# Plain writes in the two turns of the substituted blocks, strided reads in what uses them

## The reference

```
def step(s, inp):                       # one token, one head
    r_t, w_t, k_t, v_t, kk_t, a_t = inp
    sa = einsum('bhvk,bhk->bhv', s, -kk_t)
    s = s * w_t + sa * (kk_t * a_t) + v_t * k_t
    return s, einsum('bhvk,bhk->bhv', s, r_t)
```

## Time and profile before

| | |
|---|---|
| median of three runs | 4666.56 us (4660.83 to 4667.1) |
| profiled execution, its own time | 4672.97 us |
| its span | 4671.2 us |
| mean granted clock of TensorE | 0.863 of full speed |
| PE busy, matmuls | 3689.4 us, 79% |
| DVE busy | 1769.3 us, 38% |
| ACT busy | 776.1 us, 17% |

### The profile page before, as it was taken

How to read it: one execution, slowest core, us unless ns; L and a number is a source line. 1 busy time by engine, 2 the same in 40 slices (tenths; PEclk the granted TensorE clock), 3 DMA queues, 4 the chain that set the end, 5 groups by cost and what they waited for, 6 DMA issues and landing times. The chain is left out here.

```text
span 4671.2 us, 51101 instructions
## 1 busy us (share of the span) xinstructions
PE 3689.4 (79%) x21012; PEld 2181.8 (47%) x21012; DVE 1769.3 (38%) x3454; ACT 776.1 (17%) x1454; POOL 60.1 (1%) x77
## 2 busy tenths in 40 slices
PE   5788778877877888886997577785978879758995
PEld 2355445544655545544443432233444444437884
DVE  2466655665563646644001300002142321332112
ACT  1223222322230211111000100001121121200011
POOL 0000000000000000000000000000000000000000
PEclk7888788888867998988998599996989999867997
DMA  3110110011101010003102599972010000026884
GB/s 130 74 51 15 64 64 35 30 64 51 45 20 51 27 48 34 27 28 153 54 36 81 197 428 428 428 316 103 39 75 36 38 36 39 36 78 259 334 330 166
DMA packets 73151, 530.80 MB, mean 114 GB/s; under 512 B 23248, under 2 KB 24656, under 8 KB 46096
## 3 DMA queue, kind: packets, MB, share of 16 engines
q1 hardware_dynamic: 66064, 503.01, 27.1%
q0 software_dynamic: 4608, 16.78, 1.0%
q10 hardware_dynamic: 2304, 8.39, 0.4%
HBM read 500.81 MB, written 27.34 MB: 113 GB/s over the span
## 5 line engine op out<-in xcount | busy, mean ns | idle before, releaser
L1740 PE MATMUL ex_ps<-ex_ring,ex_xs 128*64 128x512 f32 x1024 | 241.1, 626 | 66.7 <-DMA ex_ring<-expert_slabs_in 63.7
L2477 PEld LDWEIGHTS ge_ps<-ge_xeT,ge_ring 128*128 128x128 f32 x2048 | 233.7, 194 | 10.5 <-issue 10.5
L2477 PE MATMUL ge_ps<-ge_xeT,ge_ring 128*128 128x128 f32 x2048 | 234.0, 277 | 2.9 <-DVE ge_xeT L2535 2.9
L1974 PE MATMUL mh_ps<-mh_w,xmT 128*128 128x512 f32 x512 | 223.1, 596 | 8.6 <-ACT mh_sg L1997 8.6
L692 PE MATMUL rw_ps<-hT,rw_w 128*128 128x512 f32 (+1 forms) x560 | 218.0, 535 | 0.0
L1125 PE MATMUL sg_ps<-hTp,sg_w 128*128 128x512 f32 x384 | 180.7, 626 | 27.9 <-PEq L61 27.9
L1740 PEld LDWEIGHTS ex_ps<-ex_ring,ex_xs 128*64 128x64 f32 x1024 | 87.3, 144 | 220.0 <-issue 218.1
L1974 PEld LDWEIGHTS mh_ps<-mh_w,xmT 128*128 128x128 f32 x512 | 97.6, 191 | 133.5 <-issue 121.5
L528 PE MATMUL rw_ps<-rw_tk,cs 128*2 128x512 f32 (+2 forms) x384 | 152.6, 560 | 0.0
L692 PEld LDWEIGHTS rw_ps<-hT,rw_w 128*128 128x128 f32 x560 | 104.8, 196 | 77.0 <-issue 68.4
L1965 PE MATMUL mh_ps<-xmT,mh_w_ahead 128*128 128x512 f32 x256 | 120.7, 636 | 22.5 <-PEq L61 22.5
(11 more groups left out here) (584 smaller groups left out, 5902.4 us busy)
## 6 DMA issues: line engine op xcount, KB each, us to landing
ex_ring<-expert_slabs_in SPq DMA_DIRECT2D x96, 2048.0 KB, 17.3
ge_ring<-expert_slabs_in SPq DMA_DIRECT2D x48, 2048.0 KB, 13.1
rw_tk<-mod_w_in SPq DMA_DIRECT2D x8, 3072.0 KB, 15.4
rw_tk<-ada_in SPq DMA_DIRECT2D x8, 2048.0 KB, 9.3
mh_w_ahead<-head_slabs_in SPq DMA_DIRECT2D x8, 2048.0 KB, 10.8
mh_w<-head_slabs_in SPq DMA_DIRECT2D x8, 2048.0 KB, 10.3
rw_w<-rw_slabs_in SPq DMA_DIRECT2D x8, 1536.0 KB, 6.5
sg_w<-xbc_slabs_in SPq DMA_DIRECT2D x4, 3072.0 KB, 10.4
```

Source lines behind the costliest of these rows:

```text
L1740: mm = pe.matmul(ps[halves[j], bank, :], src[:, k, halves[j]], ring[:, (n + j) % RING, k, :], start=k == 0, stop=k == KC - 1)
L1974: mm = pe.matmul(ps[:, 4 + t, :], xmT[:, k, P * t:P * t + P], w[1 + n // 4][:, k, :], start=k == 0, stop=k == KC - 1)
L2477: mm = pe.matmul(ps[:, 2 + 2 * (j % 2) + n, P * f:P * f + P], w[:, k, P * f:P * f + P], xeT[:, j, k, :], start=k == 0, stop=k == KC - 1)
```

## The change

Both turns write in plain order: `by_row` is now indexed `[c, u]` and `by_col` `[i, u]`, and everything that reads one unit of them reads with a stride of 32 numbers. The number of instructions, their order, their waits and their results are the same.

```
-  mm = pe.matmul(ps[hi, bank, ...], near[lo, u, 32:64], by_row[lo, u, :], start=True, stop=True)
+  mm = pe.matmul(ps[hi, bank, ...], near[lo, u, 32:64], by_row[lo, :, u], start=True, stop=True)
...
-  mm = pe.matmul(ps[lo, 5, at], mid[hi, u, :], by_col[hi, u, :], start=True, stop=True)
+  mm = pe.matmul(ps[lo, 5, at], mid[hi, u, :], by_col[hi, :, u], start=True, stop=True)
...
-  mm = pe.matmul(ps[hi, 5, at], by_col[hi, u, :], mid[hi, u, :], start=True, stop=True)
+  mm = pe.matmul(ps[hi, 5, at], by_col[hi, :, u], mid[hi, u, :], start=True, stop=True)
...
-  act.copy(xt[quarter(x), of_dir(d), quarter(x % 2)], src[quarter(x), of_dir(d), :]).then_inc(s.xt_ready, 1)
+  act.copy(xt[quarter(x), of_dir(d), quarter(x % 2)], src[quarter(x), :, of_dir(d)].rearrange("p i u -> p u i")).then_inc(s.xt_ready, 1)
...
-  dve.transpose(by_row[:, :, :].rearrange("p u c -> p c u"), xb[:, :, :].rearrange("p i c -> p c i")).then_inc(s.turned, 1)
-  dve.transpose(by_col[:, :, :].rearrange("p u i -> p i u"), xb[:, :, :]).then_inc(s.turned, 1)
+  dve.transpose(by_row[:, :, :], xb[:, :, :].rearrange("p i c -> p c i")).then_inc(s.turned, 1)
+  dve.transpose(by_col[:, :, :], xb[:, :, :]).then_inc(s.turned, 1)
```

More of the change, by code:

```diff
@@ L743, in _ @@
                         bank = 7 if u < 16 else 4
-                        mm = pe.matmul(ps[hi, bank, 32 * (u % 16):32 * (u % 16) + 32], near[lo, u, 32:64], by_row[lo, u, :], start=True, stop=True)
+                        mm = pe.matmul(ps[hi, bank, 32 * (u % 16):32 * (u % 16) + 32], near[lo, u, 32:64], by_row[lo, :, u], start=True, stop=True)
                 mm.then_inc(s.mid_done, 1)
```

## The result

The changed kernel takes 4709.65 us (median of 4 runs, 4696.48 to 4713.67), the kernel before 4666.14 beside it (4 runs, 4660.83 to 4667.1): ratio 1.0085, interval 1.0070 to 1.0100. It is slower by 43.5 us. The forecast was slower by 20, with a range that ends at 4730. The direction is as forecast, and so is each mechanism that was in the sum; the size is not.

A forecast was written before the change was run, and what follows sets the result against it. PE was taken as the chain in seven runs, ACT in the last. Joins 17.6 us in seven runs, last run 0.2 (PE) and 2.3 (ACT), turns 0: +20 us, median 4687 us, range 4661 to 4730.

The forecast's parts named there:

- PE is the chain, the turns are covered: Seven recurrence runs with projections: PE reaches the first join 7.3 us after the turns, so nobody is late because of them.
- The turns: DVE's two turns per run: plain writes save 0.8 to 1.6 us a run, all covered, worth 0 on the path.
- The copies: ACT's eight strided copies into rw_xt: 2.3 us a run more, hidden in seven runs, exposed in the last (0 to 4.5).
- The joins: PE's matmuls reading the turned tiles with a stride: 2.5 us a run more, 17.6 us in seven runs.
- the floor of 25 ns: Quoted skill rule for PE that matmuls never start closer; the joins would cost 5.5 us in seven runs, 8 in all.
- the stride is paid once a column: Value taken for PE's joins: 29.1 ns a record, 13.1 more than 16.0; forecast 4687 us, chance 0.48.
- The last run's joins: Last run, PE at low clock: only 2.5 ns a record on top for join two's 96, 0.2 us.
- The clock in the scan: Scan after the joins: clock falls in two of seven runs, 4.64 us each; not in the sum.
- PE pays for each cycle: Rival in the joins: strided number fetched twice per column, 57 us in seven runs, 62 in all, 4729 us; chance 0.14.
- PE does not feel the stride: Rival in the joins: two cycles a column cover the fetch, 4669 us; with the 25 ns floor case, chance 0.30.
- The clock is kept: Rival in the scan: shifted starts keep full clock in the two falling runs, 9.3 us faster, 4657; chance 0.08.

The follow-up runs named there:

- e3: Kernel before plus two extra plain turns; PE and ACT wait for all four, nobody reads with a stride: 4671.71 us against 4668.47, ratio 1.0009.
- e5: Measurement kernel: extra PE matmul series, ACT copies and DVE additions differing only in operand step (1 to 32), put before the first join; executed once, 4934.97 us.
- e2: Kernel before plus two extra plain turns; only ACT's eight copies read with the stride, joins read the old tiles: 4677.81 us against 4668.47, ratio 1.0018.
- e4: Kernel before, no stride; join one issued twice, join two one and a half times, 2.3 us a run more on PE: 4704.67 us against 4668.47, ratio 1.0086.
- e10: Kernel before, no stride; join one issued three times, join two twice, 4.6 us a run more on PE: 4747.03 us against 4668.76, ratio 1.0167.
- e6: Kernel before, no stride; four of ACT's eight copies moved behind its copies of the first join's result: 4670.69 us against 4667.0, ratio 1.0012.
- run 1: Not a changed kernel: one of the recurrence's eight runs, one per pair of heads, with projections; in e10 it loses clock, but not in the scan.

## Why the prediction was right or wrong

- **PE is the chain, the turns are covered: right.** No idle time stands ahead of L744 in either profile, and e3 doubled the turns for nothing that could be told from none.
- **The turns: right within the bounds.** L909 fell from 2002 to 1226 ns, as its twin L898 said. L908 came to 1946, near the bound at which the strided read is paid (2005). Both are worth nothing.
- **The copies: right, a little low.** 0.79 us was forecast, 0.86 measured: 0.92 ns an element more, not 0.74. ACT copies plain elements faster than DVE adds them (in e5, 1048 against 1225 ns for 1024), and both come to about the same when strided (2016 and 1960). The right way to say it is a rate and not a surcharge. In the last run the copies are exposed, as forecast: 2.6 us for 2.3. e2 puts all that hangs on them at 9.3 us (4.2 to 12.6), its own extra turns included.
- **The joins: right, a little high.** 29.1 ns from record to record was forecast, 28.0 measured ((2.89 - 0.23) / 95); the sum per run is 2.25 us where 2.5 was forecast. Moving and stationary operand pay alike: 42 records of L753 and 42 of L755 are 1.36 us each. The prediction also set L744's 16.0 ns against the floor of 25 ns that it quotes. The 16.0 ns are between records, and two records make a matmul, so matmuls start 32 ns apart. The trace refutes the floor for records alone; a floor of 25 ns for whole matmuls would bind neither kernel. That the stride is paid once a column, and not once a cycle, was the choice between ends 57 us apart, and it held.
- **The last run's joins: right.** 2.91 us for 2.77 in L744, at the low clock.
- **The clock in the scan: the step that failed.** The prediction had read the fall of the clock in two of seven scans, priced it at 4.64 us, and wrote that "five runs have nothing to win, and the same mechanism can cost: all seven at 56.04 would be 23 us more". It then put it into the sum at zero, as scatter of either sign, and gave the rival that gains by it 0.08. With joins longer by 2.25 us it came out on one side: four scans fell instead of two. All falls together are 12.4 us between the profiles; between the medians about 24 us are left for them, more than any term that was in the sum. e4 shows that it needs no stride. The end that the prediction had named, all seven scans at 56.04, was reached by no kernel: e10, with twice the addition, keeps the clock in all seven scans and pays behind the joins. That 4709.65 still lies in the stated range is owed to the room left for a PE that pays for each cycle, which it does not: for this term it is luck.
- **The rivals.** "PE does not feel the stride" and "PE pays for each cycle" fall by L744's 2.89 us (1.7, and 5 or more, were their marks). "The clock is kept" looked at the right place, the scan, with the wrong sign.

What stays open: why the added time makes the clock fall, and where. In the profiles of the kernels with up to 2.3 us more, the clock falls about 2 us after the scan's first step, in serial steps (DVE's L944 and PE's products in turn) in which PE starts eight records of 64 columns in 0.53 us, 66 ns each, where L734 starts one every 29.5 ns. The same steps run through at the full clock in the other runs. In run 3 of the changed kernel and in e10's seven runs it falls at the end of a join or behind it instead, and each of these eight scans keeps it. The runs show no rule that says for one run whether and where it falls. Moving the scan by a length without adding PE work ahead of it was not tried.

## What to carry to other kernels

Before an operand is laid out so that its reader strides, multiply the reader's numbers by the strided rate and ask which engine is the chain: here a few microseconds of a covered DVE were traded for 16 us of an uncovered PE. Where a stage on the chain loses the full clock in some of its repetitions and not in others, added PE time ahead of it is not to be priced at its own length: here it cost 1.6 to 2.3 times that, and a row that shows such a fall belongs in the sum, with a sign, and not in the scatter. Count the falls, and look where they lie: a mean clock of a stretch doesn't say it (e10), and one profiled execution gives 0 to 3 of them for the same joins. A shortened wait can be outweighed by a fall in the same execution (e6); whether it causes the fall was not shown.

## What the runs showed of the hardware that was not expected

- **One rate for strided reads on three engines.** PE: 28.0 ns for a record in the pair of halves, x 2 / 32 columns = 1.75 ns a number. ACT: a plain element costs (578 - 360) / 256 = 0.85 ns in L864 and L865 (which read PSUM), plus 0.92, 1.77. DVE: L908 against L909 is (1946 - 1226) / 1024 = 0.70, on top of (751 - 484) / 256 = 1.04 for a plain element (L451, 512 against 256 elements; the slope in the earlier trace rows is 1.08), about 1.75. What looked like three different surcharges is, within these numbers, one rate.
- **The step from free to full lies between 2 and 4** on ACT and DVE (a step of 2 costs 9% and 1%), and 4 costs slightly more than 32 (ACT 2082 against 2016 ns, DVE 2035 against 1960). The Trainium skill (SBUF — State Buffer, Door 1: The DMA port swizzle) says that one can stride "4 fp32" for free; e5 disagrees, 2082 ns against 1048.
- **At PE's low clock the stride costs almost nothing** (2.91 us against 2.77 for the 96 records of L744), so PE's part of the same change would have been near free in a stage that never gets the full clock.
- **A long series of small matmuls can lose the full clock too.** In e5 it fell 5.4 us into series of 32 by 32 matmuls and in e10's run 1 5.5 us after the first join began, with PE idle for 0.5 and 0.98 us in between. In the first joins of the other kernels' runs with projections, 3.2 us at the longest, it did not fall.
